# The latents' up projection done in three passes of split weights that come through the common weight ring, in a one-core transformer block

## The reference

```
h    = rmsnorm(x, g_attn)
proj = h @ w_in                                   # 2048 x 5008
c_q, c_kv, k_rope, q_d, k_d, v_d, q_i, k_i, w_i = split(proj)
q    = rmsnorm(c_q,  g_cq)  @ w_uq                # 512 x 1536: 8 heads of 192
kv   = rmsnorm(c_kv, g_ckv) @ w_ukv               # 256 x 2048: 8 heads of 128 + 128
q, k = rmsnorm per head, last 64 columns rotated by position
y_a  = softmax(q k^T + chunk mask) v              # latent attention
y_b  = sparse attention: an indexer picks 64 keys per query, then softmax with a bias
x    = x + concat(y_a, y_b) @ w_o
x    = x + peer(rmsnorm(x, g_ffn))                # 16384 experts, product keys
```

## Time and profile before

| | |
|---|---|
| median of 3 runs | 1670.87 us (1669.01 to 1672.43) |
| the profiled execution, its own time | 1671.05 us |
| its span in the trace | 1669.3 us |
| PE busy | 1656.0 us, 99% |
| DVE, ACT, POOL busy | 61%, 30%, 17% |
| TensorE clock granted, mean over the span | 1.00 |
| the slots with the up projection | 72.0 to 141.1 us of the span |

### The profile page before, as it was taken

The page is one execution under the profiler, slowest core; times in us unless marked ns, Lnnn a source line. Parts: engine busy times, 40 slices in busy tenths (PEclk is TensorE's granted clock), DMA queues, the critical chain, the costliest instruction groups (busy, mean ns, idle before and its releaser), DMA issues.

```text
span 1669.3 us, 28850 instructions
## 1 busy us (share of the span) xinstructions
PE 1656.0 (99%) x11438; PEld 1570.3 (94%) x11438; DVE 1020.8 (61%) x1709; ACT 504.0 (30%) x1347; POOL 280.1 (17%) x252
## 2 busy tenths in 40 slices
PE   9999999999999999999999999999999999999999
PEld 7768888888999999999999999999999999999998
DVE  5426695767778999867777767753444333433333
ACT  6547567656551000035444454410000000000000
POOL 1020000000003222312212122222112211221110
PEclk9999999999999999999999999999999999999999
DMA  9674445465648999999999999999999999999996
GB/s 355 226 149 125 139 135 193 139 225 201 224 159 334 421 397 419 411 392 420 395 422 420 421 401 422 422 421 421 421 421 417 417 415 421 422 417 419 421 415 237
DMA packets 107056, 569.90 MB, mean 341 GB/s; under 512 B 11280, under 2 KB 13456, under 8 KB 48208
## 3 DMA queue, kind: packets, MB, share of 16 engines
q1 hardware_dynamic: 56768, 216.22, 34.5%
q0 software_dynamic: 31792, 220.50, 32.9%
q10 hardware_dynamic: 18432, 132.41, 19.2%
HBM read 563.04 MB, written 4.46 MB: 340 GB/s over the span
## 4 chain that ended last, share of the span: by engine, by line
PE 85%; DMA 9%; DVE 2%; issue 1%; ACT 1%; POOL 1%; ACTq 0%; DVEq 0%
PE ps L1580 31%; PE ps L1525 25%; PE ps L1318 6%; PE ps L1320 5%; PE ps L1319 5%; DMA late<-in_u_rows,sel 4%; DMA sel<-sel 3%; DMA raw<-in_v_tab 2%; PE ps L1337 2%; PE ps L1474 2%; PE ps L1476 2%; PE ps L1475 2%; PE ps L1542 1%; DVE w_lo L821 1%; PE ps L1441 1%
## 5 line engine op out<-in xcount | busy, mean ns | idle before, releaser
L1145 DVE SCALAR_TENSOR_TENSOR acts<-late,sel,acts 128x2048 f32<-128x2048 f32 x77 | 181.1, 2352 | 248.6 <-DMA late<-in_v_tab,sel 248.3
L1525 PE MATMUL ps<-acts,late 128*128 128x160 f32 x2048 | 287.8, 300 | 0.0
L1525 PE MATMUL ps<-acts,raw 128*128 128x160 f32 x2048 | 287.6, 300 | 0.0
L1580 PE MATMUL ps<-acts,raw 128*128 (+1 forms) x2048 | 283.8, 299 | 1.0 <-DMA raw<-in_v_tab 0.7
L1580 PE MATMUL ps<-acts,late 128*128 (+1 forms) x2048 | 284.2, 299 | 0.0
L1580 PEld LDWEIGHTS ps<-acts,raw 128*128 128x128 f32 x2048 | 279.8, 190 | 1.9 <-issue 1.9
L1525 PEld LDWEIGHTS ps<-acts,late 128*128 128x128 f32 x2048 | 280.5, 190 | 0.0
L1525 PEld LDWEIGHTS ps<-acts,raw 128*128 128x128 f32 x2048 | 280.4, 190 | 0.0
L1580 PEld LDWEIGHTS ps<-acts,late 128*128 128x128 f32 x2048 | 280.1, 190 | 0.1
L821 DVE TENSOR_TENSOR w_lo<-raw,w_hi 128x512 fp32r<-128x512 f32 (+1 forms) x288 | 189.5, 683 | 132.8 <-ACT w_hi L544 130.6
L544 ACT ACTIVATE w_hi<-raw 128x512 fp32r<-128x512 f32 (+1 forms) x288 | 171.0, 622 | 89.0 <-PE ps L1320 42.8
(11 more groups left out here) (224 smaller groups left out, 1609.2 us busy)
## 6 DMA issues: line engine op xcount, KB each, us to landing
raw<-in_w_in SPq DMA_DIRECT2D x72, 512.0 KB, 3.5
raw<-in_u_tab SPq DMA_DIRECT2D x33, 1024.0 KB
late<-in_u_tab SPq DMA_DIRECT2D x33, 1024.0 KB
raw<-in_v_tab SPq DMA_DIRECT2D x32, 1024.0 KB
raw<-in_v_tab ACTq DMA_DIRECT2D x32, 1024.0 KB
late<-in_v_tab SPq DMA_DIRECT2D x32, 1024.0 KB
late<-in_v_tab ACTq DMA_DIRECT2D x32, 1024.0 KB
raw<-in_u_tab ACTq DMA_DIRECT2D x31, 1024.0 KB
```

The costliest lines, as they stand in the source:

```text
L1145: V.scalar_tensor_tensor(acc, row[n % NROW], w_sp[:, n - N_OWN:n - N_OWN + 1], acc, ALU.mult, ALU.add).then_inc(row_used, 1)
L1525: ins = mm(ps[:, q, 0:N_DN], ring[q][:, k * P:k * P + P], hF[:, k, :], start=k == 0, stop=k == KD - 1)
L1580: ins = mm(ps[:, pair_bank(k // 2), at:at + N_DN], ring[q][:, k * P:k * P + P], acts[:, ds(i * (4 * N_DN) + q * N_DN, N_DN)], start=first ...
```

## The change

- The latents are kept in two parts: ACT writes `lat_hi`, DVE the new `lat_lo` (six instructions).
- The weights of the up projection are no longer held whole. They are ten units of the ring: six of `w_uq` (three column blocks, each in two halves of its 512 rows) and four of `w_ukv`. Unit i comes ahead of the `w_in` unit of slot 5 + i. POOL's six DMAs are gone; SP issues ten instead.
- PE does the up projection of both token blocks at once, 12 products for a unit, three passes.
- ACT copies a column block out in the slot after its last unit, and the squares, the first root and the first rotation stand in later slots.

```diff
+    N_UP, UP_AT = 10, 5
+    B_WO = B_IN + U_IN + N_UP
-        UP_AT = 4
-        SQ_FIRST = {8: (0, 0, 0), 9: (0, 0, 4), 12: (0, 1, 0), 13: (0, 1, 4), 15: (1, 0, 0), 16: (1, 0, 4), 19: (1, 1, 0), 20: (1, 1, 4)}
-        ROOT_AT = (13, 20)
-        ROPE_AT = (15, 22)
+        UP_UNITS = [(n, k) for n in range(3) for k in (0, 2)] + [(n, 0) for n in range(3, 7)]
+        def stream(s):
+            return 16 + s + min(max(s - UP_AT + 1, 0), N_UP)
+        def up_stream(i):
+            return 16 + UP_AT + 2 * i
+        SQ_FIRST = {11: (0, 0, 0), 12: (0, 0, 4), 13: (1, 0, 0), 14: (1, 0, 4), 16: (0, 1, 0), 17: (0, 1, 4), 18: (1, 1, 0), 19: (1, 1, 4)}
+        ROOT_AT = (17, 20)
+        ROPE_AT = (18, 22)
         QPAD_AT = (18, 23)
         KROT_AT = (19, 24)
...
+            for s in range(16):
+                i = up_before(s)
+                if i is not None:
+                    n, k = UP_UNITS[i]
+                    src = w_uq[:, k:k + 2, 512 * n:512 * n + 512] if n < 3 else w_ukv[:, :, 512 * (n - 3):512 * (n - 3) + 512]
+                    load(up_stream(i), up_stream(i), src)
+                n, j = W_IN_ORDER[2 + s // 8], s % 8
+                load(stream(s), stream(s), win[:, 2 * j:2 * j + 2, 512 * n:512 * n + 512])
...
-            for i in range(6):
-                pool.wait_ge(piece_used, 10 + 4 * i)
-                dst, src, k = (w_uq, io["w_uq"], i) if i < 4 else (w_ukv, io["w_ukv"], i - 4)
-                pool.dma_start(dst[:, k, :], src[k * P:k * P + P, :]).then_inc(wu_in, 16)
...
+                if up_before(s) is not None:
+                    split_hi(up_stream(up_before(s)), up_stream(up_before(s)))
+                split_hi(stream(s), stream(s), width(W_IN_ORDER[s // 8 + 2]) if s < 8 * (N_IN - 2) else PIECE)
...
-                        dve.wait_ge(sq_done, 16 * (b + 1))
+                        dve.wait_ge(sq_done, 24 + 8 * b)
...
-                for k in range(ks):
-                    ins = mm(ps[:, bank, :], src[:, k, b * P:b * P + P], w[:, k, :], start=k == 0, stop=k == ks - 1)
+                for kk in range(2):
+                    k, part = k_first + k0 + kk, (2 * u + kk) % NPART
+                    pe.wait_ge(lo_done, 2 * u + kk + 1)
+                    for b in range(TT):
+                        t = slice(b * P, b * P + P)
+                        mm(ps[:, up_bank[b], :], lat_hi[:, k, t], whi[part][:, :], start=k == k_first, stop=False)
+                        mm(ps[:, up_bank[b], :], lat_hi[:, k, t], wlo[part][:, :], start=False, stop=False)
+                        ins = mm(ps[:, up_bank[b], :], lat_lo[:, k, t], whi[part][:, :], start=False, stop=k == k_last)
```

More of the change, by code:

```diff
@@ L92, in build_block @@
             wlo = [split_sb(f"w_lo{i}", [P, PIECE]) for i in range(NPART)]
+            over_acts = split_sb("over_acts", [P, A_LAT])
+            lat_hi = split_sb("lat_hi", [P, 6, SEQ])
+            lat_lo = split_sb("lat_lo", [P, 6, SEQ])
         late = sb("late", [P, 2 * KD * SEQ + 2 * NPART * PIECE])
@@ L179, in build_block @@
         row = [region(A_ROW, D)] + [late[:, (2 + i) * D:(3 + i) * D] for i in range(4)]
-        ring = [raw_all[:, 2 * UNIT * i:2 * UNIT * i + 2 * UNIT] for i in range(2)] + [late[:, 2 * UNIT * i:2 * UNIT * i + 2 * UNIT] for i in range(2)]
+        raw_half = [raw_all[:, 2 * UNIT * i:2 * UNIT * i + 2 * UNIT] for i in range(2)]
+        ring = [raw_half[(B_U // 2 + i) % 2] for i in range(2)] + [late[:, 2 * UNIT * i:2 * UNIT * i + 2 * UNIT] for i in range(2)]
         idx = sel[:, 0:N_PICK].bitcast(U32)
@@ L316, in build_block, with latent_gain @@
         SIDE_END = SIDE_T2 + len(groups) - N_EARLY
+        def latent_gain(k):
+            gain = G_CQ + k if k < 4 else G_CKV + k - 4
+            return gains[:, gain:gain + 1]
         def side_bank(x):
@@ L372, in _ @@
                 load(8 + j, j, win[:, 2 * j:2 * j + 2, 512:1024])
-            with sp.Fori(7, N_IN - 1) as n:
-                for j in range(8):
-                    load(n * 8 + (j - 40), j, win[:, 2 * j:2 * j + 2, ds(n * 512, 512)])
+            w_uq, w_ukv = io["w_uq"].rearrange("(k p) n -> p k n", p=P), io["w_ukv"].rearrange("(k p) n -> p k n", p=P)
+            for s in range(16):
[6 more added lines that the diff above has]
+                load(stream(s), stream(s), win[:, 2 * j:2 * j + 2, 512 * n:512 * n + 512])
             for j in range(8):
-                load(32 + j, j, win[:, 2 * j:2 * j + 2, 512 * (N_IN - 1):IN_W])
+                load(stream(16 + j), stream(16 + j), win[:, 2 * j:2 * j + 2, 512 * (N_IN - 1):IN_W])
             with sp.Fori(2, 7) as n:
                 for j in range(8):
-                    load(n * 8 + (24 + j), j, win[:, 2 * j:2 * j + 2, ds(n * 512, 512)])
+                    load(n * 8 + (24 + N_UP + j), N_UP + j, win[:, 2 * j:2 * j + 2, ds(n * 512, 512)])
             wo = io["w_o"].rearrange("(k p) n -> p k n", p=P)
@@ L655, in _ @@
                 for k in LATENT_T.get(s - 1, ()):
[L656 to L661, removed]
-                    side_out(SIDE_UP + g, dst, ps[:, side_bank(SIDE_UP + g), :])
+                    act.wait_ge(side_mm, k + 1)
+                    nc.scalar.activation(lat_hi[:, k, :], ps[:, side_bank(k), 0:SEQ], ACT.Copy, scale=latent_gain(k)).then_inc(latent_hi, 1)
+                i = up_before(s - 1)
+                if i is not None and (i % 2 or i >= 6):
+                    n = UP_UNITS[i][0]
+                    for b in range(TT):
+                        dst = qm[b][:, n * 512:n * 512 + 512] if n < 3 else kv[b][:, (n - 3) * 512:(n - 3) * 512 + 512]
+                        if b:
+                            act.wait_ge(piece_used, 2 * up_stream(i) + 2)
+                        side_out(SIDE_UP + TT * n + b, dst, ps[:, side_bank(SIDE_UP + TT * n + b), :])
                 if s in SQ_FIRST:
                     b, kind, h0 = SQ_FIRST[s]
-                    act.wait_ge(side_done, SIDE_UP + 7 * b + (3, 7)[kind])
+                    act.wait_ge(side_done, SIDE_UP + (5, 13)[kind] + b)
                     for h in range(h0, h0 + 4):
@@ L959, in _ @@
             for s in range(SLOTS):
-                split_lo(16 + s, s, width(W_IN_ORDER[s // 8 + 2]) if s < 8 * (N_IN - 2) else PIECE)
+                if up_before(s) is not None:
+                    split_lo(up_stream(up_before(s)), up_stream(up_before(s)))
+                split_lo(stream(s), stream(s), width(W_IN_ORDER[s // 8 + 2]) if s < 8 * (N_IN - 2) else PIECE)
                 if s in FIRST_AT:
@@ L971, in _ @@
                         V.tensor_scalar(proj[b][:, O_CKV:O_CKV + CKV], proj[b][:, O_CKV:O_CKV + CKV], rs_c[:, 2 + b:3 + b], None, ALU.mult).then_inc(cn_done, 1)
+                for k in LATENT_T.get(s - 1, ()):
+                    dve.wait_ge(latent_hi, k + 1)
+                    V.scalar_tensor_tensor(lat_lo[:, k, :], ps[:, side_bank(k), 0:SEQ], latent_gain(k), lat_hi[:, k, :].bitcast(F32),
+                                           ALU.mult, ALU.subtract).then_inc(side_done, 1)
                 if s == 4:
@@ L1410, in _ @@
                         pe.wait_ge(proj_done, pos - 1)
-                    tall_unit(16 + s, j, 2 * j, pos % 2, width(W_IN_ORDER[pos]), j == 0, j == 7)
+                    if up_before(s) is not None:
+                        up_unit(up_before(s))
+                    tall_unit(stream(s), stream(s), 2 * j, pos % 2, width(W_IN_ORDER[pos]), j == 0, j == 7)
                 else:
```

74 lines of the change are left out of this document (37 added, 37 removed).

## The result

| | median us (lowest to highest) | ratio to before, 95% interval |
|---|---|---|
| before | 1670.9 (1669.0 to 1672.4) | |
| after | 1678.9 (1676.6 to 1684.0), 5 runs | 1.0056 [1.0045, 1.0067] |
| forecast | 1673.1 (1666.5 to 1677.0) | |

What follows compares the result with a forecast made beforehand. PE, busy for 1656.0 of 1669.3 us, was taken as the bound. The profiled 1671.05 less 7.6 of PE's work, plus waits of 5.1 and 4.8, gave 1673.3, or 1673.1 us at the median; range 1666.5 to 1677.0.

Steps and rivals of the forecast that it cites:

- What bounds the kernel: Whole kernel: PE, busy for 1656.0 of 1669.3 us, so only its own work or its waits change the time.
- the first wait: Ahead of slot 19: PE waits 5.1 us for DVE's block of reciprocal, rotation and rotated queries before the low parts.
- The second wait: Slot 11: PE waits 4.8 us for a weight unit that loads beside the earlier burst of bias reads.
- the sum: Whole kernel: 1671.05 - 7.6 + 5.1 + 4.8 = 1673.3 us, given as 1673.1 at the median.
- Rival D: Slots 11 and 12: the contended stretch feeds on itself from four contended units, price 8.6 us, total 1677.0; chance 0.17.
- Rival B: Weights take turns with the bias, so only DVE's wait at slot 19 remains: 1668.4 us; chance 0.22.
- A unit's price under contention: Beside the bias reads: each weight unit takes 2.8 us of the DMA engines, 5.6 us for two.
- PE's own work: Slots 5 to 18: fp32r passes replace 34.4 us of float32 products by 27.2 us; PE's work falls by 7.6 us.
- The bound of 0.5 us: Margin on PE's work in the changed stretch: no reason seen to go lower or higher by more than 0.5 us.
- The sign against me: Slots 12 to 16: a PE wait caused by ACT's squares, 5.2 us in a slot of 5.44, counted as none.
- E: The products with the latents' parts don't run at 0.227 us, perhaps at float32 pace: 1697 us with both waits; chance 0.03.
- C: Neither new wait happens, leaving only PE's saving: 1670.9 - 7.6 = 1663.3 us; chance 0.08.

Runs made afterwards that it cites:

- e2: The changed kernel with POOL's 16 bias reads spread out, one for four pieces PE has used, instead of in a burst: 1671.2 us.
- e5: The kernel before, float32 up projection kept, with only the changed tables for squares, first root and first rotation: 1679.3 us.
- e4: The changed kernel with unread filler products on PE, sixteen ahead of slot 11's products and eighteen ahead of slot 19's: 1677.4 us.
- e7: The changed kernel with the bias reads spread over PE's pieces and eighteen unread filler products at the start of slot 19: 1670.8 us.
- e10: The changed kernel with each 128 KB bias read contiguous and written to 128 partitions by 1 KB instead of 16 by 8 KB: 1672.0 us.
- e3: The changed kernel with token block 0's steps apart again (rotation slot 14, rotated queries 15) and the bias reads spread out: 1666.8 us.
- e6: The changed kernel with each partition's 8 KB of bias read as one contiguous piece instead of 8 skewed rows, still 16 partitions: 1681.7 us.
- e11: The changed kernel with the bias reads taken from 16 places of the expert table v, 8 KB rows, still to 16 partitions: 1681.5 us.
- e8: The changed kernel with bias reads spread out, block 0's steps apart, rotation in slot 13, rotated queries in 14, one unneeded wait dropped: 1663.7 us.
- e1: The changed kernel with only the tables edited, token block 0's squares, root, rotation and rotated queries in separate slots again: 1672.7 us.

## Why the prediction was wrong

**What bounds the kernel, and the first wait: right.** PE waits for DVE's block ahead of slot 19, forecast 5.1 us, measured 4.99. The working holds in its parts. It had the block's start 1.4 us ahead of the end of slot 18's transposes (8.8 against 10.2), and it stands 1.7 ahead (141.97 against 142.65 + 1.03); it had 5.8 us for the block, and it takes 6.1 (to 148.05). In e2 the same wait is 5.0 us.

**The second wait: right in cause and place, in size partly by luck.** Forecast 4.8 us in slot 11, measured 3.9 there and 0.9 in slot 12, where the sum had nothing ("after that units come faster than PE wants them"). The bias came 11.3 us earlier on the clock (87.21 against 98.46), 10.1 when the 1.2 us by which this execution was ahead at that point are taken off; forecast 10.4. But I counted two contended units in 17 us. Five, issued from 88.92 to 101.19, landed after 10.3 to 16.6 us, and in the 20 us from 88 SP moved 1.98 MB, against 1.05 in the 17 of before. The unit that PE wanted in slot 12, issued at 97.72, had landed by 112.3 and was split only at 114.89, behind the late unit before it and ACT's copies and squares of slot 11. That 3.9 and 0.9 add up to the forecast is luck. Rival D, a stretch that feeds on itself for 8.6 us, thus had its condition, four contended units, but not its price in this execution. Rival B, that the weights take turns with the bias, had a rule of the Trainium skill for it (page "DMA: Bandwidth & Descriptors", section "Queues, rings and completion order"); the landings of 10.3 to 16.6 us show that turns in the queue did not protect SP. A unit's price under contention from the earlier trace rows, 2.8 us of the engines, was sound (in after 47.1% of 20 us for 1.98 MB, an estimated 2.5); why it is so high, the 16 partitions, I did not ask.

**PE's own work: 1.4 us less saved than forecast.** I had 63.7 us from the first product of slot 5 to the end of slot 18's unit. In e2, where nothing waits in it, that stretch is 65.1 us (70.90 to 136.00), against 71.3 before (71.83 to 143.15): 6.2 us saved, not 7.6. The 120 products with the latents go at 0.233 us and the other wide ones at 0.229, not at the 0.227 of the earlier trace rows; three narrow units with the steps between them take 6.9 instead of 6.5 us. The bound of 0.5 us that I gave for it was too tight.

**The step that failed is the sum.** "1671.05 - 7.6 + 5.1 + 4.8 = 1673.3" prices a wait of PE at its own length. PE hadn't waited for more than 0.2 us in this part of the kernel before, the windows there showed no clock but 1.00, and I took that clock for granted on the other side of two waits of 4 and 5 us. The runs showed 3.3 us more there: in after as products at half their pace with a clock of 0.58, in e5 the same after one wait, and in e4 and e7, where PE is kept busy in the wait, it is gone although the weights' low parts come no earlier (first product behind the wait at 107.77 in e4 against 108.04, at 141.97 in e7 against e2's 142.03).

The trace of before did hold this price, at its start, in the pace of the products and not in the clock column, which says 1.00 there. Behind a wait of 2.15 us they stand 0.43 us apart (twelve of them from 8.02 to 13.28, the first 0.56):

```profile
8.02 0.77 PE L1318 MATMUL ps<-w_hi,hT_hi 128*128 128x512 f32 x1 [2.15 <-DVE w_lo L821]
...
13.28 0.63 PE L1318 MATMUL ps<-w_hi,hT_hi 128*128 128x512 f32 x1
```

The stage from the `lat` transposes to the indexer's dots, by its parts:

| term | forecast us | measured us |
|---|---|---|
| PE's own work | -7.6 | -6.2 |
| wait for DVE | +5.1 | +5.0 |
| waits for weights | +4.8 | +4.8 |
| slow clock behind both | not in the sum | +3.3 |
| not accounted for | | +0.6 |
| stage | +2.3 | +7.5 (114.2 to 121.7) |

The rest of the profiled execution gave 2.0 us back: 0.8 behind the stage and 1.2 ahead of it. The 1.2 is the slow clock as well, by chance: at the start of the kernel the products at 0.43 us cost 2.9 us in before and in e10, 1.6 in after, under 0.1 in e3 and e5, behind waits of 2.2 to 3.2 us (in after the clock from 9 to 12 us is 0.51, in e10 0.50). Hence 1676.6.

The median of five lies 2.3 us higher still. The waits of the other four executions weren't seen, but their clock was: its mean is 0.997, 0.997, 0.995, 0.995 and 0.994 for 1676.6, 1678.2, 1678.9, 1681.2 and 1684.0 us. And the price of the clock isn't fixed. From the first product of slot 19 to the transposes behind slot 20 PE takes 5.7 us in e4 and 5.8 in e7; with the wait of 5.0 us ahead of it, it takes 7.3 in after, 7.6 in e2, 7.7 in e10, 8.0 in e6 and 8.5 in e11:

```profile
150.01 0.70 PE L1347 MATMUL ps<-w_hi,hT_hi 128*128 128x400 f32 x1 [4.99 <-DVE w_lo L844]
...
158.53 0.71 PE L1481 MATMUL ps<-ident,acts 128*128 128x128 f32 x5
```

The same wait costs 1.5 to 2.8 us more than its length (7.3 - 5.8, 8.5 - 5.7), and the execution of after that was profiled is at the low end. That dearer clock, and longer waits, make up the 2.3 us is likely and not shown: runs of kernels that starve scatter (after 7.4 us, e6 5.3 us) more than e2's (3.2) and e8's (0.6), but e10, which doesn't wait for weights, has 5.8. Of the 5.8 us between forecast and median the slow clock, 3.3, is the largest term that was seen; the smaller saving is 1.4.

**What the prediction's last part asked for.** PE's waits name DVE's low parts at slot 19 and in slot 11, ACT waited for a DMA into `raw` (6.18 us at 106.54), units took over 10 us: all found. The sign against me, a wait in slots 12 to 16 that ACT's squares cause, came in part: they stand in the chain ahead of the 0.9 us in slot 12, behind a late unit. The products with the latents ran at their fp32r pace (against E). C was reachable: it is e8, 1663.7, against its 1663.3, though the stage is only 5.9 us shorter there (108.3 against 114.2) and the rest came from ahead of it and behind it.

## What to carry to other kernels

On TensorE a new wait can cost more than it lasts: where it would stand still for 4 or 5 us, add the time of the products behind it at the lower clock, here another 1.5 to 2.8 us a wait. Look for that price in the trace you have, by the distance of the products behind any wait. Before work on the bounding engine is made shorter, look at what is timed by its progress: here a table that is read when the 48th piece is done came 10 us earlier, into the weights of the very stage that had been sped up; pacing it by the consumer's counter cost nothing and took the wait away. And two steps that other engines do between a bounding engine's pieces shouldn't be put into one slot, though their sum over the stage is small: e1 and e8 have the same work as after, and only its places differ.

## What the runs showed of the hardware

- After each of ten waits of PE of 3.5 to 6.3 us (after, e1, e2, e5, e6, e10, e11) the granted clock of the 3.5 us from its restart was 0.50 to 0.55, and the products behind cost 1.5 to 2.8 us more than at 1.00. The wait of 1.6 us in e3 and those of up to 0.9 us in e4 left it at 1.00. At the start of the kernel, after ten products of 256 columns, waits of 2.2 to 3.2 us were followed by products at half pace in eleven of thirteen executions, and by none in e3 (2.5 us) and e5 (2.2 us).
- The clock column can miss it: in before it says 1.00 from 8 to 14 us, where the products up to 13.7 us stand 0.43 us apart instead of 0.23.
- Sixteen transfers of 128 KB to 16 partitions each, with the weights beside them, held the windows of 4 us from 92 to 108 at 165 to 224 GB/s with all DMA engines busy (share 0.99 to 1.08). With 128 partitions each it was 345 to 359 GB/s from 92 to 104. The 512 KB of a weight unit issued from 88 on landed in 9.4 to 18.4 us in the first case (issued up to 104), in 3.6 to 7.0 in the second.
- So a DMA share of 1.0 doesn't tell how many bytes are moved.
